# Fewer prefix products, later loads and reordered lists between routing and experts, in a hybrid decoder layer

## The reference

```
h2 = rmsnorm(x, norm_ffn)
coarse = softmax(h2 @ w_coarse)            # 4 groups; the best one is kept
fine   = (h2 @ w_fine)[its group]          # 4 experts; the best two are kept
top_w  = softmax(top two of fine) * g_prob # a token's share of each
out    = sum over its experts of ((silu(g) * u) * share) @ w_down[e],  g, u = split(h2 @ w_up[e])
x      = x + out
```

## Time and profile before

| | |
|---|---|
| median of 3 runs | 539.82 us (539.28 to 540.59) |
| the profiled execution: its time by the profiler, first to last instruction (span) | 539.0 us |
| PE busy | 511.2 us (95%) |
| DVE busy | 394.0 us (73%) |
| ACT busy | 280.2 us (52%) |
| GpSimd busy | 176.5 us (33%) |
| mean granted TensorE clock | 0.976 |

### The profile page before, as it was taken

How to read it: one execution, slowest core, us unless ns; L and a number is a source line. 1 busy time by engine, 2 the same in 40 slices (tenths; PEclk the granted TensorE clock), 3 DMA queues, 4 the chain that set the end, 5 groups by cost and what they waited for, 6 DMA issues and landing times.

```text
span 539.0 us, 7480 instructions
## 1 busy us (share of the span) xinstructions
PE 511.2 (95%) x2622; PEld 414.8 (77%) x2622; DVE 394.0 (73%) x658; ACT 280.2 (52%) x457; POOL 176.5 (33%) x348
## 2 busy tenths in 40 slices
PE   6999999999999999999999999779999999999992
PEld 3888877778778877878888888777887877777761
DVE  4889774997979979767558524568988878788740
ACT  5634144555655565643343212245767777877741
POOL 1229948689599000000000000032213232324344
PEclk9999999999999999999999999957999999999997
DMA  8560551122022101242587737579999999966433
GB/s 309 70 215 3 146 167 30 50 79 78 2 80 78 46 16 58 60 116 61 151 291 281 291 134 296 194 229 411 377 327 327 319 358 369 344 235 172 123 45 38
DMA packets 62775, 93.95 MB, mean 174 GB/s; under 512 B 14183, under 2 KB 45959, under 8 KB 62738
## 3 DMA queue, kind: packets, MB, share of 16 engines
q1 hardware_dynamic: 56304, 80.84, 43.9%
q0 software_dynamic: 5184, 8.41, 7.1%
q10 hardware_dynamic: 1250, 4.22, 2.0%
HBM read 88.19 MB, written 12.58 MB: 187 GB/s over the span
## 4 chain that ended last, share of the span: by engine, by line
PE 76%; DVE 7%; POOL 5%; SPq 4%; DMA 3%; issue 2%; ACT 2%; POOLq 0%; DVEq 0%; ACTq 0%
PE pj L1730 10%; PE pj L1732 9%; PE pj L1731 9%; PE pj L2103 6%; PE pj L2104 5%; PE pj L2105 5%; PE m L2124 5%; PE tp L2089 3%; SPq L511 2%; PE m L2129 1%; PE m L2131 1%; PE m L2130 1%; PE pj L1847 1%; PE m L1730 1%; PE sc L1822 1%
## 5 line engine op out<-in xcount | busy, mean ns | idle before, releaser
L1730 PE MATMUL pj<-h_high,split 128*128 128x512 f32 x192 | 76.6, 399 | 0.2 <-DVE h_low L1422 0.2
L1732 PE MATMUL pj<-h_high,split 128*128 128x512 f32 x192 | 74.9, 390 | 0.0
L1731 PE MATMUL pj<-h_low,split 128*128 128x512 f32 x192 | 74.8, 390 | 0.0
L612 POOL TENSOR_TENSOR rstd<-ssq,half_col 128x1 f32<-128x1 f32 x8 | 4.4, 556 | 184.7 <-DVE ssq L1094 171.1
L1603 DVE TENSOR_TENSOR up_low<-arena_front,up_high 128x2048 fp32r<-128x2048 f32 x23 | 52.7, 2292 | 11.2 <-ACT up_high L971 11.2
L2103 PE MATMUL pj<-up_high,xt_high 128*128 128x512 f32 x128 | 51.4, 402 | 0.9 <-DVE xt_low L1637 0.9
L2104 PE MATMUL pj<-up_low,xt_high 128*128 128x512 f32 x128 | 51.0, 398 | 0.0
L2105 PE MATMUL pj<-up_high,xt_low 128*128 128x512 f32 x128 | 50.8, 397 | 0.0
L971 ACT ACTIVATE up_high<-arena_front 128x2048 fp32r<-128x2048 f32 x23 | 44.2, 1928 | 10.8 <-PE pj L2105 9.7
L712 POOL DMA_INDIRECT out_dram<-arena_back,idx_all x12 | 23.6, 1964 | 64.4 <-DMA out_dram<-arena_back,idx_all 46.7
L412 ACT ACTIVATE split<-arena_front 128x2048 fp32r<-128x2048 f32 (+1 forms) x20 | 34.7, 1739 | 18.4 <-PE sc L1732 10.9
(11 more groups left out here) (348 smaller groups left out, 1324.6 us busy)
## 6 DMA issues: line engine op xcount, KB each, us to landing
arena_front<-in_w_expert_up_dram SPq DMA_DIRECT2D x23, 1024.0 KB, 12.2
arena_back<-in_w_expert_down_dram SPq DMA_DIRECT2D x16, 1024.0 KB, 13.0
arena_front<-in_w_in_dram SPq DMA_DIRECT2D x12, 1024.0 KB, 5.6
arena_back<-in_w_expert_up_dram SPq DMA_DIRECT2D x9, 1024.0 KB, 13.5
arena_front<-in_w_out_dram SPq DMA_DIRECT2D x4, 1024.0 KB, 5.0
arena_back<-in_x_dram SPq DMA_DIRECT2D x4, 512.0 KB, 6.4
arena_front<-in_w_ssm_glu_gate_dram SPq DMA_DIRECT2D x8, 256.0 KB, 2.9
arena_front<-in_w_ssm_glu_val_dram SPq DMA_DIRECT2D x8, 256.0 KB, 3.5
```

The lines of the kernel that those rows point to most:

```text
L1730: pe.matmul(dst, sh, mh, start=first and i == 0, stop=False)
L1731: pe.matmul(dst, sh, ml, start=False, stop=False)
L1732: ins = pe.matmul(dst, sl, mh, start=False, stop=last and i == len(terms) - 1)
```

## The change

1. PE: the six products with the matrix of ones become three. Each takes the choice of one earlier tile, repeated by a broadcast access pattern, for all later tiles at once (48, 32 and 16 columns).
2. SP: halves 5 and 6 are issued behind the landing of the first gather, together with 7 to 9. The store of the last 128 residual rows moves from ACT's queue to SP's, and stands right behind that gather too, ahead of half 5.
3. ACT: the exponential of `below` comes ahead of the first two weight copies instead of behind them.
4. DVE: reading the first list (`first_list(0)`) stands between two instructions of the share chain, reading the second (`first_list(1)`) one link later.
5. DVE: `low_up(0, 1)` and `low_up(1, 0)` come ahead of `read_lists(1)`; `low_up(1, 0)` is taken out of the loop's first turn.
6. PE: the lists of experts 2 and 3 come between the two halves of `up(0)`, and those of experts 4 and 5 behind `turn_rows(1)`.

```diff
 # SP
             piece_used(sp, P_OUT + 2)
-            load_half(5)
-            for t in range(TT):
-                sp.wait_ge(h2_stored[t], 16)
-            load_half(6)
             sp.wait_ge(gathered[0], 16)
-            for i in range(7, 10):
+            sp.wait_ge(x2_done, 4 * TT)
+            sp.dma_start(out_rows[(TT - 1) * P:TT * P, :], x2[:, TT - 1, :]).then_inc(x2_stored, 16)
+            for i in range(5, 10):
                 load_half(i)
 # ACT
-                act.dma_start(out_rows[t * P:(t + 1) * P, :], x2[:, t, :]).then_inc(x2_stored, 16)
+                if t < TT - 1:
+                    act.dma_start(out_rows[t * P:(t + 1) * P, :], x2[:, t, :]).then_inc(x2_stored, 16)
...
+            act.wait_ge(r_dve, 1)
+            act.activation(below, below, ACT.Exp).then_inc(r_act, 1)
             high_up(0, 0)
             high_up(0, 1)
-            act.wait_ge(r_dve, 1)
-            act.activation(below, below, ACT.Exp).then_inc(r_act, 1)
             high_rows(0)
 # DVE
             for e in range(2):
                 pick_list(e)
-            for e in range(2):
+            def first_list(e):
+
                 v.wait_ge(idx_full, e + 1)
                 ts(idx_all[:, e:e + 1], sc[e][:, 128:129], float(SEQ), None, ALU.add).then_inc(first_idx, 1)
 
             v.wait_ge(r_act, 1)
             E4 = below.rearrange("p (t g) e -> p t g e", t=TT)
             mark(v.tensor_reduce(both_sums[:, 0, :], E4[:, :, 0, :], AX_X, ALU.add))
-            link(tt(kept.rearrange("p t (g e) -> p t g e", g=NG), E4[:, :, 1:, :],
+            mark(tt(kept.rearrange("p t (g e) -> p t g e", g=NG), E4[:, :, 1:, :],
                     chosen[:].bitcast(F32).rearrange("p t (g e) -> p t g e", g=NG), ALU.mult))
+            first_list(0)
+            settle()
             link(v.tensor_reduce(both_sums[:, 1, :], kept, AX_X, ALU.add))
+            first_list(1)
             link(tt(both_sums[:, 2, :], both_sums[:, 0, :], both_sums[:, 1, :], ALU.mult))
...
             low_rows(0)
+            low_up(0, 1)
+            low_up(1, 0)
             read_lists(1)
-            low_up(0, 1)
             for e in range(NE):
...
-                if e + 1 < NE:
+                if e and e + 1 < NE:
                     low_up(e + 1, 0)
 # PE
-            for t in range(TT):
-                for later in range(t + 1, TT):
-                    ins = pe.matmul(sc[0][:, later * NE:(later + 1) * NE], ones[:], chosen[:, t, :], start=False, stop=t == TT - 2)
+            for t in range(TT - 1):
+                later = TT - 1 - t
+                ins = pe.matmul(sc[0][:, (t + 1) * NE:TT * NE].rearrange("p (t e) -> p t e", e=NE), ones[:],
+                                chosen[:, t:t + 1, :].broadcast_to([P, later, NE]), start=False, stop=t == TT - 2)
...
             turn_rows(0)
+            up(0, range(DC // 2))
             pe.wait_ge(idx_done, 1)
             place_lists(LISTS[1], LISTS[2])
-            for e in range(NE - 1):
+            up(0, range(DC // 2, DC))
+            turn_rows(1)
+            pe.wait_ge(idx_done, 2)
+            place_lists(LISTS[2], LISTS[3])
+            for e in range(1, NE - 1):
                 up(e, range(DC))
                 if e < LAST_LISTS:
                     pe.wait_ge(idx_done, e + 2)
                     place_lists(LISTS[e + 2], LISTS[e + 3])
-                if e:
-                    turn_act(e - 1)
+                turn_act(e - 1)
                 turn_rows(e + 1)
-                if e:
-                    down_(e - 1)
+                down_(e - 1)
```

## The result

The changed kernel took 544.0 us in the median of 11 runs (540.5 to 547.24), the kernel before 539.82 in 11 runs beside it. The ratio is 1.0068 with a 95% interval of 1.0048 to 1.0087. So it is slower by about 0.7%, where the prediction had 538.0 with a range of 536.5 to 540.0. The profiled execution took 542.54 us, of which 540.7 are its span (539.0 before). The spans of the two traces are thus 1.7 us apart, the medians 4.2: this one trace shows where time goes, but less than half of the loss.

The account below looks back on a forecast made before the run. TensorE, busy 511.2 of 539.0 us, was taken as the bound. The steps were summed on the path to `up(1)`, starting 1.8 us earlier (weighed from 1.55 and 2.1): 539.82 - 1.8 = 538.0 us, range 536.5 to 540.0.

Parts of the forecast that it names:

- 1, products: PE's prefix products ahead of the first gather: three of six fall away, 0.55 to 0.63 us gained, 0.63 taken.
- 2, gather: First gather without half 6 issued ahead of it: gain taken as 0, at most 0.6 us.
- 2, loads: Halves 5 to 9 issued later on SP: still in time, with ten us of slack, growing.
- Rival C: Final adds: 6 us more transport in the full stretch delays them 1 to 3 us; 538.3 to 539.8; chance 0.09.
- 3 and 4, exponential and shares: ACT's exponential and DVE's share chain before the experts: copies' delay hidden, chain ends near 356.0, 0 on the path.
- 5, lists: PE's lists moved into and behind `up(0)`: `up(1)` starts earlier, weighed gain 1.8 us, including the earlier gather.
- rival D: Early clock rise in `up(0)`, or a faster gather: gain 3.05, with up to 0.6; 536.2 to 537; chance 0.12.
- 6, DVE order: DVE's subtractions ahead of the list read: no loss; gather 2 issued about 369.2, slack 1.9 us.
- Rival B: Gather 2 held behind DVE's subtraction: stall 0.8 to 2.7 us ahead of `turn_rows(2)`, slower; chance 0.09.
- Rival A: Gain ahead of `up(1)` only partial, 0 to 1 us, from old clock-rise time or DVE's list wait; chance 0.22.

Follow-up runs that it names:

- e2: Kernel before with only halves 5 and 6 and the last residual rows' store moved behind the first gather on SP; 543.45 us, ratio 1.0065.
- e6: Kernel before with only the six products replaced by three broadcast products; 539.08 us, ratio 0.999.
- e3: Changed kernel with half 5 alone put back at its old place; half 6 and the store stay late; 539.35 us, ratio 0.9992.
- e4: Changed kernel with the store of the last residual rows back on ACT's queue; halves 5 and 6 stay late; 540.49 us, ratio 1.0012.
- e13: Changed kernel with down weights 4 to 15 issued from ACT's queue instead of SP's; 544.84 us, ratio 1.0088.
- e1: Changed kernel with halves 5 and 6 and the residual store back where the kernel before had them; 537.69 us, ratio 0.9964.
- e8: Kernel before with the three products, the exponential ahead of the copies and the list reads within the share chain; 538.99 us, ratio 0.9986.
- e5: Changed kernel with each pair of up halves issued one expert later, behind down weights; 541.59 us, ratio 1.0033.
- e12: e1 with down weights 4 to 15 issued from ACT's queue instead of SP's; 539.56 us, ratio 1.0008.

## Why the prediction was wrong

By the prediction's own steps (its numbers 1 to 6):

- **1, products: right.** 0.63 us forecast. From the first count product to the first gather it is 5.11 us before and 4.47 after: 0.64. e2 and e6, which differ in step 2 besides the products, have the same two values.
- **2, gather: right.** The landing took 4.37 us instead of 4.62 (a gain of 0 forecast, 0.6 at most). But that is within the scatter: without half 6 ahead of the gather e2, e3, e4 and e13 have 4.44, 4.50, 4.29 and 4.64, with it e1, e6 and e8 have 4.66, 4.41 and 4.58. Gather 0, issued 0.9 us ahead of DVE's subtraction, took 1.29 us and wasn't held; gather 1, issued within it, took 2.50.
- **2, loads: this failed.** The step said of the halves "ten us of slack, growing". Half 5 landed at 366.9 (365 forecast) and was used at 374.1: 7.2 us, and the slack of the later up halves did grow, to 27 us for half 15, before it shrank again to 10.5 for half 30. (The 1.4 us to the first bytes in that sum stand in no row that the prediction shows; in the trace before, half 5's first packet starts 1.0 us after its issue.) But I looked only at the loads that I moved. The loads that were short were the down weights of experts 9 to 12, a hundred us later and untouched by the edit. Before the change the slack of the down weights already shrank, from 25.5 us for expert 4 to 6.9 for expert 12. The prediction gave their wait no term.
- **Rival C: right cause, wrong victim, size too small.** It named 6 us more transport in the full stretch, let them go to the adds and priced them at 1 to 3 us, leaving 538.3 to 539.8. The traces show the loss at the weights. The sum that was missing is: smallest slack 6.9 us, less 6 us of transport moved, less the gain itself, since an earlier PE wants its weights earlier. With the forecast terms that is 6.9 - 6 - 1.8 = -0.9: half of the gain gone, 538.9, and still no loss. What makes it a loss is that the 6 us were too small. The down weight of expert 12 landed 9.1 us later, more than its whole slack of 6.9, so ACT reads it 2.2 us later than before (499.83 against 497.60) and any lead is lost by then. With use 3.95 us earlier the sum is 6.9 - 9.1 - 3.95 = -6.2, and PE's stall brings a slow clock with it.
- **3 and 4, exponential and shares: right.** The chain of shares ended at 354.87; 356.0 forecast less the 1.07 of this execution is 354.9. Nothing waited for it, and e8 shows no more than step 1's gain.
- **5, lists: right in size, and the larger traced gain was luck.** The list products took 0.8 us in the middle of `up(0)`. The clock rose 3.6 us after the start, near the early end of what I had weighed, where the trace before has 6.1. That makes 2.85 us between these two traces, near rival D's 3.05; at like delays the change gains 1.55 to 1.9, which is the 1.8 of the forecast. The early rise belongs to the execution and not to the change: e2, with the lists as before, has it too (2.9 us).
- **6, DVE order: right.** Gather 2 was issued at 367.31 (369.2 less 1.07, that is 368.1, forecast), landed at 375.54, and `turn_rows(2)` began at 377.68 without a wait: 2.1 us of slack (1.9 forecast). Rival B didn't happen.
- **Rival A** didn't either: the local gain was whole.

What is measured by runs is that step 2 costs 0.65% alone, that its cost grows with the amount moved (the intervals of e3 and e4 overlap), that another order of the loads (e5) gives back about half of it, and that another queue (e13) gives back nothing. What stays open: why the landings fall 9 us behind when the bytes had nearly caught up at 400 us, why a load's shares drift apart (below), and how much of the store's 0.56% is its place. The traced gain of e1 (4.5 us of span) is also larger than that of its runs (0.36%, 1.9 us). Its profiled execution, 536.52 us, was the second fastest of its 12 and had the clock back 3.0 us after the start of `up(0)`, so one trace overstates it.

## What to carry to other kernels

Before moving a load out of an idle time, take the slack of every load behind it up to the end, not only of those moved, and look for the smallest. If it is less than the moved transport plus the time gained, part of the gain is paid back there; if it is less than the delay of the landing alone, the kernel gets slower. Leave a margin, since that delay was 9.1 us here where the transport was 6 to 7.6. A DMA share near 1.0 for a hundred us, and a time from issue to landing that rises from load to load (7.5 us for expert 4's down weight, 23.6 for expert 12's, before), were the sign that such a stock was being used up. And before a gain between two traces is put down to a change, look whether the clock rose at the same point in both. A cheap test is to put the loads back and keep the rest, which here gave the best version.

## What the runs showed of the hardware

- **The 16 shares of a load drift apart.** In the kernel before, a down weight issued at 385.9 had its first share landed after 4.6 us and its last after 7.5; one issued at 467.2 after 5.3 and 23.6. The last share sets the landing. I read it as a DMA engine whose queue falls behind under loads, gathers and adds; no run tested that, and the trace doesn't tell which engine a packet ran on. The Trainium skill, DMA: Bandwidth & Descriptors, section "Why a DMA increments its semaphore by 16 and not by 1", says that the engines of one DMA finish independently and each adds one. The increments in these traces agree.
- **Issuing stops being free.** The issue of expert 11's down weight on SP takes 0.37 us in the kernel before and 9.71 in the changed one. All of SP's issues from 355 us on take 15.5 us in the kernel before (37 of them), 22 in e1 and 105 in the changed kernel (40). I read it as a queue that is full. While SP hangs there, the quicker DMA engines may run dry, which would fit the share of 0.93 in 400 to 440; no run tested that.

```profile
457.46 0.37 SPq L548 DMA_DIRECT2D arena_back<-in_w_expert_down_dram  x1
```

```profile
457.42 9.71 SPq L548 DMA_DIRECT2D arena_back<-in_w_expert_down_dram  x1
```

- **The clock's return isn't a fixed delay.** With the same order of PE's work from the count products to `up(1)`, the granted clock went from 0.50 to 1.00 (1.2 to 2.4 GHz) 3.0 us after `up(0)` began in e1, 3.6 in the changed kernel, 4.8 in e3, 6.1 in e4 and 6.2 in e12. A second fall came behind the 2.49 us wait that ended at 492.86, and cost about 2 us more: from the transposes of expert 13 to those of expert 14 it is 14.24 us instead of 9.73.
